# Every third weighted sum beside the two attention fronts on VectorE instead of TensorE

## The reference, cut to what matters

```python
best_s, best_pos = lax.top_k(cand_s, PEER_TOPK)
expert = jnp.take_along_axis(cand_i, best_pos, axis=-1)
gate = jax.nn.softmax(best_s, axis=-1)
u_sel = jnp.take(u, expert, axis=0)
v_sel = jnp.take(v, expert, axis=0)
act = jax.nn.gelu(jnp.einsum('btd,bthkd->bthk', hx, u_sel, ...), approximate=False)
return jnp.einsum('bthk,bthkd->btd', (gate * act).astype(h.dtype), v_sel)
...
h = h + peer(rmsnorm(h, norm_ffn[layer]), ...)
```

## Time and profile before

| | us |
|---|---|
| median of 3 runs | 2488.28 |
| lowest and highest | 2478.59, 2488.97 |
| the profiled execution's own time | 2487.36 |
| its span, first to last instruction | 2485.6 |
| PE busy, DVE busy | 1982.1, 1413.1 |
| ACT busy, POOL busy | 576.7, 1027.1 |

### The profile page before, as it was taken

The page is one execution under the profiler, slowest core; times in us unless marked ns, Lnnn a source line. Parts: engine busy times, 40 slices in busy tenths (PEclk is TensorE's granted clock), DMA queues, the critical chain, the costliest instruction groups (busy, mean ns, idle before and its releaser), DMA issues.

```text
span 2485.6 us, 21257 instructions
## 1 busy us (share of the span) xinstructions
PE 1982.1 (80%) x6918; PEld 1101.4 (44%) x6918; DVE 1413.1 (57%) x3068; ACT 576.7 (23%) x1204; POOL 1027.1 (41%) x1063
## 2 busy tenths in 40 slices
PE   6756767767898789768877887688877799897998
PEld 3641222222333335423344463243322297676996
DVE  0138788755344554694455447855555455555884
ACT  1111100100112431011134211111100134453663
POOL 0025656766444454464444545656666400000000
PEclk9888989999998889999988899999999899998999
DMA  3257989999889789989966899999999744353653
GB/s 146 85 168 309 371 314 367 369 368 356 320 301 345 272 285 393 348 305 357 396 235 234 329 385 346 343 370 409 396 364 368 284 144 154 111 153 103 187 182 122
DMA packets 194843, 707.96 MB, mean 285 GB/s; under 512 B 21784, under 2 KB 23072, under 8 KB 194480
## 3 DMA queue, kind: packets, MB, share of 16 engines
q0 software_dynamic: 152064, 553.72, 59.6%
q1 hardware_dynamic: 40960, 150.65, 17.9%
q10 hardware_dynamic: 1712, 2.24, 0.3%
HBM read 704.81 MB, written 1.06 MB: 284 GB/s over the span
## 4 chain that ended last, share of the span: by engine, by line
PE 54%; DVE 17%; issue 10%; DMA 7%; POOL 6%; ACT 3%; another core or an unknown queue 1%; ACTq 0%; SPq 0%; DVEq 0%; POOLq 0%
PE ps L494 22%; PE ps L652 15%; DMA a<-in_peer_u,eidx 7%; PE ps L411 5%; PE ps L426 5%; DVE a L1435 4%; POOL a L349 3%; POOL a L344 3%; DVE diag L1444 1%; DVE a L1369 1%; PE ps L444 1%; PE ps L397 1%; PE ps L598 1%; DVE a L1375 1%
## 5 line engine op out<-in xcount | busy, mean ns | idle before, releaser
L494 PE MATMUL ps<-a,diag 128*128 128x512 f32 (+1 forms) x2112 | 1091.9, 657 | 356.2 <-DVE diag L1444 237.2
L494 PEld LDWEIGHTS ps<-a,diag 128*128 128x128 f32 (+1 forms) x2112 | 402.9, 203 | 994.2 <-issue 623.0
L1435 DVE SCALAR_TENSOR_TENSOR a<-a,ps 128x1024 f32<-128x1024 f32 x512 | 622.3, 1216 | 347.3 <-DMA a<-in_peer_u,eidx 289.3
L344 POOL DMA_INDIRECT a<-in_peer_u,eidx x528 | 522.5, 990 | 636.7 <-DVE a L1435 303.4
L349 POOL DMA_INDIRECT a<-in_peer_v,eidx x528 | 503.8, 954 | 303.3 <-issue 133.3
L652 PE MATMUL ps<-a_r 128*128 128x256 f32 (+1 forms) x1648 | 393.8, 332 | 19.9 <-DVE a_r L1583 7.3
L932 ACT ACTIVATE gel<-dots 128x1 f32<-128x1 f32 x528 | 101.1, 201 | 1076.6 <-DVE a L1435 637.9
L652 PEld LDWEIGHTS ps<-a_r 128*128 128x128 f32 x1648 | 279.6, 192 | 52.3 <-DVE a_r L1583 8.1
L1577 DVE TENSOR_TENSOR ring_r<-wring,a_r 128x1024 fp32r<-128x1024 f32 x142 | 173.3, 1222 | 139.8 <-ACT a_r L1091 139.7
L1444 DVE TENSOR_SCALAR diag<-cstc,gel,a 128x128 f32<-128x128 f32 (+1 forms) x528 | 186.1, 354 | 104.0 <-issue 38.9
L1091 ACT ACTIVATE a_r<-wring 128x1024 fp32r<-128x1024 f32 x142 | 149.4, 1053 | 82.3 <-PE ps L652 82.2
(11 more groups left out here) (218 smaller groups left out, 1299.1 us busy)
## 6 DMA issues: line engine op xcount, KB each, us to landing
wring<-in_units SPq DMA_DIRECT2D x270, 512.0 KB
a<-in_peer_u,eidx POOLq DMA_INDIRECT x528
a<-in_peer_v,eidx POOLq DMA_INDIRECT x528
cs2c<-in_cs SPq DMA_DIRECT2D x1, 1792.0 KB
a<-in_poolm SPq DMA_DIRECT2D x1, 1632.0 KB, 9.2
h<-in_xin SPq DMA_DIRECT2D x2, 512.0 KB, 4.2
bcF<-in_bc_rows SPq DMA_DIRECT2D x2, 512.0 KB, 9.3
a<-in_mem SPq DMA_DIRECT2D x1, 1024.0 KB, 4.9
```

The source lines that it names most:

```text
L344: g.indirect_dma_start(ug[:, n % NU, :], None, peer_u, bass.IndirectOffsetOnAxis(ap=eidx[:, t, k:k + 1], axis=0))\
L494: last = nc.tensor.matmul(ps[0:P, 6 + j, :], diag[:, k % 4, 0:P], vg[:, k % NV, j * 512:(j + 1) * 512], start=False, stop=False)
L1435: v.scalar_tensor_tensor(ug[:, n % NU, :], ug[:, n % NU, :], 1.0, hnm if t == 2 else ps2(4), ALU.mult, ALU.mult, accum_out=dots[:, k % 8:k ...
```

## The change

In the second and third run (slots 144 to 399), every slot whose number can be divided by three, 86 in all, is summed by VectorE. `coef` builds no diagonal for it: it multiplies gelu and gate to one column (`cgt`), waits for the v gather, and adds v rows times that column to a running row `acc` of 128x1024 in SBUF. The first such slot of a run starts from h instead of `acc`. TensorE skips these slots; its diagonals are numbered by a count of its own slots, and so is the ring of four. `sums_end` adds `acc` in the place of h after waiting for VectorE's last sum. GpSimd waits for whichever engine summed the slot that held the v buffer.

```diff
+        def on_dve(n):
+            return 16 + SLOTS <= n < 16 + 3 * SLOTS and n % 3 == 0
+        pe_slots, dve_slots = [0], [0]
+        for n in range(16 + 4 * SLOTS):
+            pe_slots.append(pe_slots[-1] + (not on_dve(n)))
+            dve_slots.append(dve_slots[-1] + on_dve(n))
...
-                if n >= NV:
-                    g.wait_ge(S("vsum"), n + 1 - NV)
+                if n >= NV and on_dve(n - NV):
+                    g.wait_ge(S("vdve"), dve_slots[n + 1 - NV])
+                elif n >= NV:
+                    g.wait_ge(S("vsum"), pe_slots[n + 1 - NV])
...
             def sums_slot(P, k, n, vfill):
-                pe.wait_ge(S("diag"), n + 1)
+                if on_dve(n):
+                    return
+                pe.wait_ge(S("diag"), pe_slots[n + 1])
                 pe.wait_ge(S(f"v{k % NV}"), vfill)
...
             def sums_end(t, m):
+                if m in (3, 4):
+                    pe.wait_ge(S("vdve"), dve_slots[16 + (m - 1) * SLOTS])
...
-                                            h[0:P, t, j * 512:(j + 1) * 512], start=False, stop=True)
+                                            acc[:, e] if m in (3, 4) else h[0:P, t, e], start=False, stop=True)
...
                 dve.wait_ge(S("gelu"), n + 1)
-                if n >= 4:
-                    dve.wait_ge(S("vsum"), n - 3)
+                if on_dve(n):
+                    d, c = dve_slots[n], slice(k % 8, k % 8 + 1)
+                    link(v.tensor_tensor(cgt[:, c], gel[:, c], gate, ALU.mult))
+                    dve.wait_ge(S(f"v{n % NV}"), 16 * (n // NV + 1))
+                    if d in (0, dve_slots[16 + 2 * SLOTS]):
+                        old = h[:, t, :]
+                        if d:
+                            dve.wait_ge(S("wo_h"), 1)
+                            dve.wait_ge(S("y_pe"), 3)
+                    else:
+                        old = acc[:, :]
+                        dve.wait_ge(S("vdve"), d)
+                    v.scalar_tensor_tensor(acc[:, :], vg[:, n % NV, :], cgt[:, c], old, ALU.mult, ALU.add)\
+                        .then_inc(S("vdve"), 1)
+                    return
+                p = pe_slots[n]
+                if p >= 4:
+                    dve.wait_ge(S("vsum"), p - 3)
```

More of the change, by code:

```diff
@@ L182, in program @@
         diag = sb("diag", [128, 4, 128])
+        cgt = sb("cgt", [128, 8])
+        acc = sb("acc", [128, D])
         poolP = a1[:, 0:4 * 3 * LTOK].rearrange("p (g s t) -> p g s t", g=4, s=3)
@@ L490, in sums_slot @@
             def sums_slot(P, k, n, vfill):
-                pe.wait_ge(S("diag"), n + 1)
+                if on_dve(n):
+                    return
+                pe.wait_ge(S("diag"), pe_slots[n + 1])
                 pe.wait_ge(S(f"v{k % NV}"), vfill)
                 for j in range(2):
-                    last = nc.tensor.matmul(ps[0:P, 6 + j, :], diag[:, k % 4, 0:P],
+                    last = nc.tensor.matmul(ps[0:P, 6 + j, :], diag[:, pe_slots[n] % 4, 0:P],
                                             vg[:, k % NV, j * 512:(j + 1) * 512], start=False, stop=False)
@@ L499, in sums_end @@
                 P = TILES[t][1]
+                if m in (3, 4):
+                    pe.wait_ge(S("vdve"), dve_slots[16 + (m - 1) * SLOTS])
                 for j in range(2):
+                    e = slice(j * 512, (j + 1) * 512)
                     last = nc.tensor.matmul(ps[0:P, 6 + j, :], ident[0:P, 0:P],
-                                            h[0:P, t, j * 512:(j + 1) * 512], start=False, stop=True)
+                                            acc[:, e] if m in (3, 4) else h[0:P, t, e], start=False, stop=True)
                 last.then_inc(S("y_pe"), 1)
@@ L1441, in coef @@
                 dve.wait_ge(S("gelu"), n + 1)
-                if n >= 4:
-                    dve.wait_ge(S("vsum"), n - 3)
-                v.tensor_scalar(diag[:, k % 4, 0:W], unit_mat, gel[:, k % 8:k % 8 + 1], gate,
+                if on_dve(n):
[16 more added lines that the diff above has]
+                    dve.wait_ge(S("vsum"), p - 3)
+                v.tensor_scalar(diag[:, p % 4, 0:W], unit_mat, gel[:, k % 8:k % 8 + 1], gate,
                                 ALU.mult, ALU.mult).then_inc(S("diag"), 1)
@@ L1605, in _ @@
             flush(1, b_base, SLOTS)
-            dve.wait_ge(S("vsum"), 16 + 4 * SLOTS)
+            dve.wait_ge(S("vsum"), pe_slots[16 + 4 * SLOTS])
             norm("n2B", [1], 14)
```

## The result

| | before | after |
|---|---|---|
| median, us | 2485.21 (5 runs) | 2471.13 (5 runs) |
| lowest and highest | 2478.59, 2488.97 | 2464.1, 2474.92 |
| span of the profiled execution | 2485.6 | 2469.4 |
| ratio with 95% interval | | 0.9939 [0.9917, 0.996] |

The change makes the kernel 14 us faster; the forecast was 38.

What follows compares the result with a forecast made beforehand. The prediction took TensorE to bound the streaming stages, VectorE the top-k stretches, both in turn the head pairs. Gains of 80.0 less 24.8 for top-k and 17.1 given back net 38.1 us: 2449 us, range 2425 to 2482.

Steps and rivals of the forecast that it cites:

- the cost on VectorE: Each moved slot: multiply, wait and 1024-wide sum replace a diagonal, adding 1.18 us a slot, 101 us in all.
- Rival D: A sum on VectorE costs more than forecast; slower from 2.5 us a slot, 2518 us at 3; chance 0.09.
- the top-k term: Top-k stretches at the fronts' ends, bound by VectorE: 21 moved slots add 11.8 and 13.0 us, 24.8 together.
- a slot that stands between units is worth its length: Streaming stages: a slot taken from TensorE saves its full 1.72 or 1.91 us, if the DMA follows.
- gains at risk: Gains in DMA-saturated stretches: o, f1, wq of both fronts and k, v, q of the second; 34.3 us.
- GpSimd's longer issues: New sums with two SBUF inputs can lengthen a gather's issue by up to 1.28 us; nothing added to the time.
- What the DMA gives back: In saturated streaming stages TensorE gets ahead of transfers; the middle of none and 34.3 us, 17.1, is given back.
- The ring of eight units: In the first front's 961 to 1017 us, this ring and the 8 v buffers cushion transfers at the edge.
- Rival B: The DMA takes all of the streaming gains, 34.3 us, leaving 20.9 us gained, 2466 us; chance 0.22.
- the head pairs: Attention's batches of three to five slots in both fronts: 7.9 and 10.8 us gained, 18.7 together.
- The late first diagonal: Head-pair batches whose first slot is VectorE's get their first diagonal 2.6 us later, so 0.7 us is lost.
- Rival E: Work moves but time doesn't: head pairs give nothing and the DMA takes the streaming gains; 2485 us, chance 0.10.

Runs made afterwards that it cites:

- only_topk: Kernel before with only the 22 slots from k = 96 on of the two fronts moved to VectorE; 2447.17 us, ratio 1.0087.
- no_topk: Changed kernel with the 22 top-k slots left on TensorE, 64 slots moved in all; 2391.4 us, ratio 0.9868.
- one_sbuf: Changed kernel whose new sums up to k = 119 take a PSUM operand in place of the running row; 2408.57 us, ratio 0.9932.
- the halved transfers: Kernel before and changed kernel, both with half weight units and half v-gather rows in the two fronts; 2420.52 and 2378.0 us, 42.5 us apart.
- streams_only: Changed kernel with VectorE's slots only outside the head pairs and the top-k; 2454.77 us, ratio 0.9874.
- the filling alone: Kernel before with 14 bf16 zero matmuls ahead of each of the 16 head-pair batches; 2468.27 us, ratio 0.9924.
- halfv_after: Changed kernel with half weight units and half-row v gathers in the two fronts; 2378.0 us, ratio 0.9806.
- light_after: Changed kernel fetching only half of each weight unit in the two fronts; 2453.06 us, ratio 0.9863.
- cs2_after: Changed kernel with the 1.8 MB constants load moved from ahead of wq's first unit to ahead of the second front's k; 2417.12 us, ratio 0.9971.

## Why the prediction was right and wrong

**Right: the direction and the cost on VectorE.** 1.18 us a slot was worked out from line 1302's 1283 ns, the small operation and the overlap; 1.13 is measured, the new sum takes 1285 ns, and no wait before it is worth naming (3.0 us in all). Rival D is out: a cost of 2.5 us would have been needed.

**Right: the top-k term.** 24.8 forecast; 21.5 by stages, 21.6 by `only_topk`, 17.6 by `no_topk`.

**Right: a slot that stands between units is worth its length** where the transfers follow: k of the first front gained 5.0 (5.7 forecast), q 3.4 in either front (3.4 each), o of the first 3.4 (3.4). The second q and the first o stood in before at a DMA share of 1.02 or 1.03, on the forecast's list of gains at risk, and kept them all the same. Also that GpSimd's longer issues are covered (`one_sbuf`).

**Wrong: the term "What the DMA gives back".** I took the middle between nothing and 34.3, 17.1; the halved transfers say 26 to 28. The middle rested on no row. Two things were wrong in that step. The sum over 961 to 1017 us set the bytes of the stage against the time TensorE needs, 21 MB against the 20 MB that 49 us bring, and called it "at the edge". It was over the edge: from the start of wq to the end of the scores the stage gained 2.0 us in the first front and 3.9 in the second instead of 6.9, and with halved transfers 6.8 in either. The ring of eight units was to cushion it; that it starts wq less full now, because the stages ahead are shorter and run at 410 GB/s, is what I take from the rows, and no run shows it by itself. And the worst that I allowed was a gain of nothing. f1 was on the list of gains at risk with 1.7 in either front, qh was not on it at all; that such a stretch can get longer than before was nowhere in the sum. The row of before between o and wq stands below 1.0 (346 GB/s). In after the same stretch runs at 410 GB/s and is longer. The reason, from the timeline of VectorE:

```profile
924.47 1.28 DVE L1472 SCALAR_TENSOR_TENSOR acc<-a,cgt,acc 128x1024 f32<-128x1024 f32 x1
928.26 1.22 DVE L1453 SCALAR_TENSOR_TENSOR a<-a,ps 128x1024 f32<-128x1024 f32 x1 [2.51 <-DMA a<-in_peer_u,eidx]
...
929.67 1.21 DVE L1555 TENSOR_TENSOR h<-h,ps 128x1024 f32<-128x1024 f32 x1
```

The dot at 928.26 has waited 2.51 us for its u rows, and behind it on the engine stands line 1555, which adds the projection to h and opens the norm. A gather that is late in a streaming stage delays one slot; here it delays the front itself. f1 came out at -1.9 and -1.7, qh at -1.2 and -3.4: 8.2 us lost where 6.8 were forecast as gained before the give-back. That f1's loss comes from this wait is read from the timeline; for qh I only infer it.

Rival B, "the DMA takes all of the streaming gains", 20.9 us, is nearer in size, and its ground, the shares of 1.02, was the better evidence: it leaves 61.3 - 34.3 = 27.0 us in the streaming stages, and 28.6 were measured. That it comes so near is in part luck, for single stages that it prices at nothing kept their gain (q, o) and others lost (f1, qh). Its total is too high by the head pairs. What spoke against it in the prediction, that TensorE idles only 2.2 of 56 us, says that the stage was not yet limited by transfers. It doesn't say that the stage had room. The limit itself was read rightly, 409 GB/s and not 358. The page that I cited, DMA: Bandwidth & Descriptors of the Trainium skill, says in its section Measured that a core alone in its pair measures up to 425 GB/s; the stretches shown here, 410 GB/s at most, agree with that better than with the limit which I quoted from it.

**Wrong: the head pairs**, 18.7 forecast and 8.7 measured. The late first diagonal was sized rightly (2.4 us, 2.6 forecast). The price of a saved slot was not: 1.87 came from the difference of a batch of four and one of three, each after the same idle time. In the first front the idle time grew by 9.6 us, more of the remaining records ran at the lower level (44 after 36), and a slot saved only 1.16; in the second 1.77. Waits within batches, costed at nothing, took 2.4 and 2.3 us, and the wait for softplus 2.2 more in the second. On the chip of the halved runs 15.4 of the 18.7 came out, with halved and with full transfers alike, so 6.7 of the missing 10.0 us belong to the chips on which the kernel before takes 2485 us. What differs there stays open.

**Rival E** had both shortfalls: it left 27.0 us in the streaming stages and nothing in the head pairs, where 28.6 and 8.7 were measured.

How the transfers' toll divides among the streaming stages stays open, for a stage's start already depends on what the one before had left in the buffers. And even with halved transfers 12.3 of the 61.3 us of the streaming terms are missing. 3.3 of them are the two last slots behind the top-k (3.4 forecast, 0.1 measured); the rest no run separates.

## What to carry to other kernels

Before work is taken off an engine that overlaps with transfers, look at the bytes of all the stages between two places where the transfers rest, and not at one stage. Here two stages at a DMA share of 1.02 or 1.03 kept their 3.4 us, and the ones beside them filled up as soon as they got shorter: qh and f1 lost 8.2 us where 6.8 were counted as gained. A gather that is late hurts most where the engine that waits for it has the critical chain's next step queued behind (2.51 us ahead of line 1555, 3.48 us ahead of the scores' eviction in `streams_only`). Gains of single edits need not add: the change alone 0.9939, the filling alone 0.9924, both 0.9923. And two slots took 6.55 us behind 5.46 us of idle time, so the price of one more or one less of a short batch's steps is not the average; in the head pairs, keeping TensorE busy was worth more (19 us) than taking work from it (8 us).

## What the runs showed of the hardware

- Fourteen matmuls of bf16 zeros (3.19 us) ahead of a batch of fp32 matmuls keep TensorE's granted clock at its higher level: 0.99 instead of 0.84 in the head pairs of the first front, 0.43 to 0.53 instead of 0.85 to 1.02 us from the start of one record to the next at the head of a batch, and 19 us less for the kernel before (`fill_before`).
- The issue of a gather by GpSimd takes 1.93 us beside a VectorE operation of 1.28 us with two SBUF inputs, and 0.93 us beside the same operation with one of them in PSUM (`after`, `one_sbuf`).
- With half rows of `peer_v` (2 KB) and half units, beside full rows of `peer_u`, the DMA share is at 1.01 with 372 GB/s (`halfv_after`), with half units alone at 1.01 with 388 (`light_after`), and with everything in full at 1.03 with 409 (after). The share says when the engines are full, the rate doesn't.
- 1.8 MB moved into a stretch at 409 GB/s made its units 7 us longer, and 5 us to the end of the scores (`cs2_after` against `no_topk`); at that rate they are 4.4 us. The rest isn't explained.
